# One matmul with 128 moving columns per block and head in the levels of a bidirectional gated scan

## The reference

```python
def gla_scan(q, k, v, log_f, s0):          # per head, chunk by chunk
    b = jnp.cumsum(gc, axis=2)
    diff = b[:, :, :, None, :] - b[:, :, None, :, :]
    decay = jnp.where(lower, jnp.exp(jnp.where(lower, diff, 0.0)), 0.0)
    scores = jnp.einsum('bhtd,bhsd,bhtsd->bhts', qc, kc, decay)
    o = scores @ vc + jnp.einsum('bhtd,bhde->bhte', qc * jnp.exp(b), s)

def bidir_scan(q, i, fwd, bwd, s_fwd, s_bwd):
    o_f, sf_out = gla_scan(q, fwd[0], i, fwd[1], s_fwd)
    o_b, sb_out = gla_scan(flip(q), flip(bwd[0]), flip(i), flip(bwd[1]), s_bwd)
    return o_f + flip(o_b), sf_out, sb_out
```

## Time and profile before

| | |
|---|---|
| time, median of 3 runs | 1816.63 us (1815.48 to 1818.06) |
| span of the profiled execution, first to last instruction | 1812.9 us |
| PE busy | 1737.4 us, 96% |
| DVE busy | 851.8 us, 47% |
| ACT busy | 687.6 us, 38% |
| HBM read | 477.56 MB |
| mixer of the odd layer, `g` = 0 to 3 | 648 to 887 us |

### The profile page before, as it was taken

How to read it: one execution, slowest core, us unless ns; L and a number is a source line. 1 busy time by engine, 2 the same in 40 slices (tenths; PEclk the granted TensorE clock), 3 DMA queues, 4 the chain that set the end, 5 groups by cost and what they waited for, 6 DMA issues and landing times.

```text
span 1812.9 us, 28102 instructions
## 1 busy us (share of the span) xinstructions
PE 1737.4 (96%) x11446; PEld 1286.0 (71%) x11446; DVE 851.8 (47%) x1206; ACT 687.6 (38%) x897; POOL 4.2 (0%) x6
## 2 busy tenths in 40 slices
PE   6999999999999999999899999999999999998988
PEld 3677677888887799989777877766536887763343
DVE  2435425434533656767569876554105555410001
ACT  4332622222224646445477755443004444400001
POOL 0000000000000000000000000000000000000000
PEclk9999999999999999999999999999999999999999
DMA  9835266433632221321169999999999999999997
GB/s 349 310 139 184 87 218 234 160 93 132 240 95 69 93 87 54 94 90 40 70 264 393 351 342 409 409 409 409 409 409 409 408 407 408 404 408 409 409 409 289
DMA packets 161986, 480.46 MB, mean 265 GB/s; under 512 B 14992, under 2 KB 58176, under 8 KB 155712
## 3 DMA queue, kind: packets, MB, share of 16 engines
q1 hardware_dynamic: 161856, 478.66, 69.5%
HBM read 477.56 MB, written 1.05 MB: 264 GB/s over the span
## 4 chain that ended last, share of the span: by engine, by line
PE 74%; DMA 12%; SPq 6%; DVE 4%; ACT 2%; issue 2%; DVEq 0%; ACTq 0%
PE ps L754 18%; PE ps L756 17%; PE ps L755 17%; SPq L701 5%; PE ps L1533 5%; DMA arena<-in_moe_up 3%; PE ps L1604 3%; DMA raw<-in_moe_up 3%; DVE w_lo L2076 2%; DMA arena<-in_moe_w 2%; PE ps L773 1%; PE ps L1522 1%; PE ps L1167 1%; PE ps L1165 1%; PE ps L1596 1%
## 5 line engine op out<-in xcount | busy, mean ns | idle before, releaser
L2076 DVE TENSOR_TENSOR w_lo<-raw,w_hi 128x1024 fp32r<-128x1024 f32 x220 | 264.8, 1221 | 268.6 <-ACT w_hi L1687 266.2
L1687 ACT ACTIVATE w_hi<-raw 128x1024 fp32r<-128x1024 f32 x220 | 229.4, 1056 | 377.6 <-PE ps L756 307.9
L754 PE MATMUL ps<-h_hi,w_hi 128*128 128x512 f32 (+1 forms) x736 | 279.2, 379 | 3.3 <-DVE h_lo L2158 2.2
L756 PE MATMUL ps<-h_lo,w_hi 128*128 128x512 f32 (+1 forms) x736 | 273.3, 371 | 0.0
L755 PE MATMUL ps<-h_hi,w_lo 128*128 128x512 f32 (+1 forms) x736 | 273.0, 371 | 0.0
L2076 DVE TENSOR_TENSOR w_lo<-arena,w_hi 128x1024 fp32r<-128x1024 f32 x114 | 137.0, 1222 | 76.9 <-ACT w_hi L1687 73.2
L754 PEld LDWEIGHTS ps<-h_hi,w_hi 128*128 128x128 f32 x736 | 138.6, 188 | 47.6 <-issue 21.5
L756 PEld LDWEIGHTS ps<-h_lo,w_hi 128*128 128x128 f32 x736 | 138.6, 188 | 24.7
L755 PEld LDWEIGHTS ps<-h_hi,w_lo 128*128 128x128 f32 x736 | 138.8, 189 | 22.6 <-issue 0.5
L1687 ACT ACTIVATE w_hi<-arena 128x1024 fp32r<-128x1024 f32 x114 | 119.3, 1059 | 93.4 <-DMA arena<-in_moe_up 45.6
L754 PE MATMUL ps<-w_hi,s_hi 128*128 128x512 f32 x336 | 135.0, 402 | 4.8 <-DVE w_lo L2076 4.7
(11 more groups left out here) (387 smaller groups left out, 2541.5 us busy)
## 6 DMA issues: line engine op xcount, KB each, us to landing
arena<-in_moe_up SPq DMA_DIRECT2D x188, 512.0 KB, 14.6
raw<-in_moe_up SPq DMA_DIRECT2D x156, 512.0 KB, 14.8
a_slots<-in_moe_up SPq DMA_DIRECT2D x104, 512.0 KB, 14.9
arena<-in_moe_w SPq DMA_DIRECT2D x98, 512.0 KB, 15.0
raw<-in_moe_w SPq DMA_DIRECT2D x78, 512.0 KB, 15.1
arena<-in_w_ada SPq DMA_DIRECT2D x35, 1024.0 KB, 5.0
raw<-in_ffn_w SPq DMA_DIRECT2D x66, 512.0 KB, 5.8
a_slots<-in_moe_w SPq DMA_DIRECT2D x48, 512.0 KB, 15.1
```

The costliest lines, as they stand in the source:

```text
L754: pe.matmul(dst, s_h, m_h, start=start, stop=False, **kw)
L756: return pe.matmul(dst, s_h, m_l, start=False, stop=stop, **kw)
L1687: act.activation(w_hi[:, o % R, :], src, ACT.Copy).then_inc(hi_done, 1)
L2076: dve.tensor_tensor(w_lo[:, o % R, :], src, w_hi[:, o % R, :].bitcast(F32), ALU.subtract).then_inc(lo_done, 1)
```

## The change

The two matmuls of a block and head become one with 128 moving columns: its columns are for every stretch the near queries of the backward direction and then the far queries of the forward one, read in turn from two places of the arena (`woven`). The two kinds of columns need different keys at each key token, near keys forward and far keys backward. ACT gathers them before each level into one tile `keys` (`level_keys`), by one copy of 128x512. The two query tiles change places so that the pattern has one positive stride. `keys` lies where `s_hi` and `s_lo` had their space, which the mixer doesn't use.

```diff
+R_TB, R_TF = R_T, R_T + G_LAT
...
         with nc.sbuf_tensor("a_parts", [P, 2, A_SIDE], F32R) as a_parts:
-            pass
+            with nc.sbuf_tensor("s_parts", [P, 2, 3072 - A_SIDE], F32R) as s_parts:
+                pass
         a_slots = sb("a_slots", [P, 2 * A_SIDE // UNIT, UNIT])
+        keys = sb("keys", [P, G_LAT])
+        s_hi, s_lo = s_parts[:, 0, :], s_parts[:, 1, :]
...
+        def woven(a, b, n, hs):
+            both = arena[:, a:a + 2 * (b + hs - a)].rearrange("p (s x) -> p s x", s=2)[:, :, 0:n]
+            return both.rearrange("p s (b c) -> p b s c", c=2 * hs)[:, :, :, 0:hs]
...
             def level(g, n):
                 b, hs = base(g), LEVELS[n]
+                pe.wait_ge(k_cp, len(LEVELS) * g + n + 1)
...
-                        dst = ps[:, 6 - n % 2, (seg * HG + h) * P:(seg * HG + h + 1) * P]
-                        pe.matmul(far(dst, hs), ar(b + R_KF + at, P), far(ar(b + R_T + at, P), hs),
-                                  start=True, stop=True, skip_group_check=True)
-                        m = pe.matmul(near(dst, hs), ar(b + R_KB + at, P), near(ar(b + R_T + G_LAT + at, P), hs),
+                        m = pe.matmul(ps[:, 6 - n % 2, (seg * HG + h) * P:(seg * HG + h + 1) * P],
+                                      keys[:, at:at + P], woven(b + R_TB + at, b + R_TF + at, P, hs),
                                       start=True, stop=True, skip_group_check=True)
...
+            def level_keys(g, n):                                   # ACT
+                b, hs = base(g), LEVELS[n]
+                if n == 0:
+                    if g > 0:
+                        act.wait_ge(l_mm, len(LEVELS) * g)
+                    act.wait_ge(k_rdy, 2 * g + 2)
+                else:
+                    act.wait_ge(l_wide, len(LEVELS) * g + n)
+                act.activation(keys.rearrange("p (b s c) -> p b s c", s=2, c=hs), woven(b + R_KF, b + R_KB, G_LAT, hs),
+                               ACT.Copy).then_inc(k_cp, 1)
...
                     split_to(high_parts(g, k))
+                    if 1 <= k < 8 and rec:
+                        level_keys(g, k - 1)
```

More of the change, by code:

```diff
@@ L281, in build @@
         h_lo = sb("h_lo", [P, KT * NT], F32R)
-        s_hi = sb("s_hi", [P, 3072 - A_SIDE], F32R)
-        s_lo = sb("s_lo", [P, 3072 - A_SIDE], F32R)
         arena = sb("arena", [P, ARENA])
@@ L389, in build @@
         b_rdy, l_wide, l_upd, l_mm, l_cp = sem("b_rdy"), sem("l_wide"), sem("l_upd"), sem("l_mm"), sem("l_cp")
+        k_cp = sem("k_cp")
         i_mul, o_mm, o_sq, o_sum = sem("i_mul"), sem("o_mm"), sem("o_sq"), sem("o_sum")
@@ L1201, in outputs @@
                     pe.matmul(dst, ar(b + R_V + HG * P + h * P, P), s1[:, h, :], start=False, stop=False)
-                    pe.matmul(dst, ar(b + R_KF + G_LAT + h * P, P), lat(b + R_T)[:, h, :], start=False, stop=False)
-                    m = pe.matmul(dst, ar(b + R_KB + G_LAT + h * P, P), ctx(b + R_T)[:, h, :], start=False, stop=True)
+                    pe.matmul(dst, ar(b + R_KF + G_LAT + h * P, P), lat(b + R_TF)[:, h, :], start=False, stop=False)
+                    m = pe.matmul(dst, ar(b + R_KB + G_LAT + h * P, P), lat(b + R_TB)[:, h, :], start=False, stop=True)
                 m.then_inc(o_mm, 1)
@@ L1240, in cross @@
                 b = base(g)
-                for d, (keys, queries) in enumerate(((lat(b + R_KF), lat(b + R_T)), (lat(b + R_KB), ctx(b + R_T)))):
+                for d, (keys, queries) in enumerate(((lat(b + R_KF), lat(b + R_TF)), (lat(b + R_KB), lat(b + R_TB)))):
                     s, t = slice(d * P, (d + 1) * P), slice((1 - d) * P, (2 - d) * P)
@@ L2382, in queries @@
                 for d in range(2):
-                    m = dve.tensor_tensor(o_part(g, d), ar(base(g) + R_Q, G_LAT),
+                    m = dve.tensor_tensor(ar(base(g) + (R_TF, R_TB)[d], G_LAT), ar(base(g) + R_Q, G_LAT),
                                           ar(base(g) + (R_LF, R_LB)[d], G_LAT), ALU.mult)
@@ L2391, in widen @@
                 dve.wait_ge(l_mm, len(LEVELS) * g + n + 1)
-                for at, (x, y) in ((R_LF, (R_KF, R_T + hs)), (R_LB, (R_T + G_LAT, R_KB + hs))):
+                for at, (x, y) in ((R_LF, (R_KF, R_TF + hs)), (R_LB, (R_TB, R_KB + hs))):
                     total = ar(b + at, G_LAT).rearrange("p (b s c) -> p s b c", s=2, c=hs)[:, :, :, 0:1]
@@ L2409, in widen_last @@
                 b = base(g)
-                for at, t, (to, by) in ((R_LF, lat(b + R_T), (1, 0)), (R_LB, ctx(b + R_T), (0, 1))):
+                for at, t, (to, by) in ((R_LF, lat(b + R_TF), (1, 0)), (R_LB, lat(b + R_TB), (0, 1))):
                     v = t[:, :, to * P:(to + 1) * P]
```

## The result

| | before | after |
|---|---|---|
| median | 1816.14 us (4 runs) | 1824.13 us (4 runs) |
| ratio | | 1.0050, 95% interval 1.0038 to 1.0062 |
| profiled execution: span | 1812.9 us | 1823.9 us |
| PE busy, instructions | 1737.4 us, 11446 | 1730.8 us, 11222 |
| ACT busy | 687.6 us | 704.0 us |

A forecast was written before the change was run, and what follows sets the result against it. PE was taken to bound the mixer, running without pause until 840 us. Groups 0 to 2 gave −1.96, −0.51 and +0.33 us, group 3 +2.9, −6.9 and +1.8: a total of −4.3, hence 1820.9 us, range 1814.5 to 1826.

The forecast's parts named there:

- the four great waits: PE idles of 5.6, 4.1 and 4.1 us before level 5 of groups 0 to 2, about 9 before level 6, group 3.
- Level 5 behind `gate_soft`: Groups 0 to 2: gather queued behind value copy, `gate_soft` and a high part; level 5 comes 4.70, 3.25, 3.25 us later.
- Level 6 behind the expert unit: Group 3: gather queued behind expert unit 0's high part, which waits for its DMA; 6.9 us lost.
- The low clock: PE at half clock after each long idle: 2.6 us lost in groups 0 and 1 each, 0.83 in group 2.
- The woven reading: Matmul columns read in turn from two places: taken as costing nothing, with 0.8 us a level kept for the range.
- rival of a slow reading: Level 0's alternating read costs 0.8 us in groups 0, 1 and 2: 1823.4 us; chance 0.18.
- The tail of group 3: From level 6 to the outputs everything as before except level 6 itself, shorter at the low clock: +1.8 us with rounding.
- The expert phase: After the mixer: moves as a whole with the mixer's end and stays as long as before.
- The other gathers: Most gathers fall mid PE slot and cost nothing; level 3 in group 3, behind L1920, costs 0.6 us.
- All of them after 840 us: Kernel before, mixer: PE's few waits (1.6, 1.9, 2.1 us) all come after 840 us; until then PE never pauses.
- The queues don't matter: Rival: ACT's gathers are in time everywhere, giving −24.9 us, 1791.7 us; chance 0.06 (or only half).
- The slow gather: Rival: a gather takes 1.0 us, so 0.4 us more at each of five places: 1822.9 us; chance 0.10.

The follow-up runs named there:

- e1: Changed kernel with the level-5 gather of groups 0 to 2 moved between the exponentials and logarithms of `gate_soft`: 1811.07 us, ratio 0.9975 to the kernel before.
- e2: Changed kernel with the level-6 gather of group 3 moved before the high part of the first expert unit: 1819.3 us, ratio 1.0017 to the kernel before.
- e4: Changed kernel, nothing moved, PE running idle matmuls before level 5 of groups 0 to 2 and level 6 of group 3: 1819.5 us, ratio 1.0022.
- b1_tail: Kernel before, with only the first expert units' high and low parts moved behind `cross_copy`: 1812.55 us, ratio 0.9983.
- e3_both: Changed kernel with level-5 and level-6 gathers moved earlier in groups 0 to 2, and level 6's in group 3: 1802.32 us, ratio 0.9922 to the kernel before.
- e5_tail: e3_both plus the first expert units' high and low parts moved behind `cross_copy`: 1796.35 us, ratio 0.9894 to the kernel before.

## Why the prediction was right

The direction, the four great waits and their mechanism were right, and the time lies inside the range. The size was not: the forecast was +4.3 us and the median moved by +8.0, and in the traces, from which the sum was made, the span moved by +11.0. The misses below that count all go the same way. That the median came closer than the span is largely luck: the sum took 3.7 us as lying around the span, and in the runs of the changed kernel that was 1.8 to 2.0 us; and the profiled execution was the slowest of its four.

- *Level 5 behind `gate_soft`.* Forecast idles of 5.6, 4.1 and 4.1 us; measured 5.46, 4.03, 4.03. From the start of slot 6 in group 0 to level 5 it was 9.35 us by the sum and 9.37 (684.18 to 693.55) in the trace. e1 shows the cause.
- *Level 6 behind the expert unit.* Forecast 8.5 us from the widening to the level, measured 8.6 (875.41 to 883.98). e2 shows the cause.
- *The low clock.* Taken at 2.6 us in groups 0 and 1. From level 5 to level 6 of group 0 the changed kernel takes 6.44 us; before it was 4.66, and with 0.9 less for the level 3.76: a loss of 2.7. e4 shows that this part is the clock.
- *The woven reading was a term taken too low.* "I take nothing": level 0 costs 0.37 us more than level 2 from start to start, and level 1's piece is 0.08 us longer. That is 0.45 us a group, about 1.4 of the 2.0 us by which the sum was already short at L1183 of group 3. The value I kept for the range, 0.8 us for level 0, was more than twice what it is. The rival of a slow reading was half true, and should have been part of the forecast. The bound had one side on a row that reads contiguous columns, which says nothing of a read in turns.
- *The tail of group 3 was short by 1.4 us up to the outputs, and by 1.7 us behind them.* The way from level 6 to the outputs took 12.6 us and not 11.8: `cross_copy` stands behind the high parts of the second and third expert units, and the DMA of the second landed 4.2 us after its issue (889.44 to 893.61), where before it was 3.6 (882.29 to 885.87). Behind them came a term that I had not written at all: the 3.45 us idle before the outputs put the clock down over them, 897.7 to 900.5, where before an idle of 2.1 us had not.
- *The expert phase* was forecast to be as long as before and was 1.6 us longer, as it was by 1.1 us and more in every trace with the woven matmul. I hadn't asked what it costs that `s_hi` and `s_lo` move.
- *The other gathers* cost nothing or, in group 3, 0.41, 0.26 and 0.83 us of waiting; I had only the first, at 0.6.
- "All of them after 840 us" was misread: in the kernel before, PE also waits 0.97 us for DVE before `cross` of group 2, at 836.4. The sum doesn't change, since it counts nothing behind 827.92 in that group.
- "The queues don't matter" fell with the first trace. The slow gather was true at levels 0 and 1 only, where ACT had time.

What is open: which property of the new place of `s_hi` and `s_lo` makes their matmuls longer, and whether that is all of the 1.6 us; why the wait before the outputs and the clock over them differ from kernel to kernel without a move at that place (e1 against the changed kernel); and how much of a single trace is chance. The runs of one kernel lie 1 to 6 us apart here, so a median and a single trace of it can differ by as much as a small effect.

## What to carry to other kernels

Work given to an idle engine costs by its place in that engine's list, not by its length: ask for every new instruction what stands before it, what that waits for, and when the consumer stands there. 28 copies of 0.6 us with ACT 38% busy cost nothing at 21 places and 24.4 us of waiting on PE at seven, 22.9 of them at four. A wait of some microseconds on PE costs a second time in clock. Seven gathers moved ahead of work that nobody needs yet turned +8 us into −13.

Look outside the part that was changed, too: a tile that only gives way to a new one can come to lie where it is read more slowly. And a forecast made from a trace is checked against a trace; which of the runs was profiled was worth 1.6 us here.

## What the runs showed of the hardware

- A 128-column fp32 matmul takes 0.22 us from start to start at 2.4 GHz with its moving columns in one piece or in turns of four and more, and 0.11 us more (0.43 over four of them) when each column is read from another place than the last; in turns of two it is 0.02 us more (0.08 over four). The 64-column matmuls of before took as long, 0.21 us each, at level 0 too, where they read every second column (1.71 us for eight).
- The same matmul can depend on where its moving columns lie. The rows of 128x512 that read `s_hi` or `s_lo` have a mean of 393 ns in before and b1_tail, and 399 to 400 ns in the changed kernel, where the two tiles lie elsewhere.
- The same holds for ACT's gather, with both ends in SBUF: 0.61 to 0.63 us from level 2 on, 0.70 at level 1, 0.84 to 0.90 at level 0, here from the changed kernel:

```profile
714.23 0.84 ACT L1905 ACTIVATE keys<-arena 128x512 f32<-128x512 f32 x1
727.00 0.70 ACT L1905 ACTIVATE keys<-arena 128x512 f32<-128x512 f32 x1 [3.31 <-DVE arena L2411]
736.48 0.61 ACT L1905 ACTIVATE keys<-arena 128x512 f32<-128x512 f32 x1
```

- The length of PE's idle alone doesn't tell what the clock does. In the mixer 1.2 and 1.7 us left it at 2.4 GHz, and each of 2.8 us and more was followed by 1.2 GHz, for 3 to 6 us of the work behind. Between them both occurred. The 1.9 us before `cross` of group 2 left it up in e3_both, and in e5_tail, at the same place, they were followed by 3.4 us at 1.2 GHz. The 1.9 us before level 6 of group 3 in the kernel before were followed by the low level, the 2.1 us before the outputs weren't.
